# A streaming trunk on one core: the table work of the state-space layer dealt out over the first expert layer in another way

## The reference, cut to what matters

```python
D_MODEL = 1024; SEQ = 256; DEPTH = 2
N_EXPERT_GROUPS = 4; EXPERTS_PER_GROUP = 8; D_EXPERT = D_MODEL // 4
for i in range(DEPTH):
    hn = rms_norm(h, norm_mix[i])
    mix = chunked_rel_attention(...) if i % 2 == 0 else s5_mixer(...)
    h = h + mix
    hn = rms_norm(h, norm_ffn[i])
    h = h + hierarchical_moe(hn, ...)     # best group, best two experts in it
return rms_norm(h, norm_final)
# in hierarchical_moe:
for e in range(N_EXPERTS):
    hid = jax.nn.silu(t @ w_gate[e]) * (t @ w_up[e])
    out = out + gates[:, e:e + 1] * (hid @ w_down[e])
# in s5_mixer: x_k = abar * x_(k-1) + bbar u_k, y = Re(C x) + D u, scan over the positions
```

## Time and profile before

| what | us |
|---|---|
| time, median of 3 runs (lowest to highest) | 711.55 (710.52 to 712.64) |
| the profiled execution | 711.8 |
| its span, first to last instruction | 710.1 |
| busy: TensorE / VectorE / ScalarE / GpSimd | 629.6 / 193.9 / 136.7 / 190.2 |
| moved by DMA | 244.20 MB, 344 GB/s over the span |
| granted TensorE clock, mean share of full speed | 0.942 |

### The profile page before, as it was taken

One profiled execution on the slowest core, in us unless ns is written; L12 is line 12 of the kernel. 1 busy time (PEld: TensorE's weight loads), 2 busy tenths in 40 slices (PEclk: granted clock), 3 DMA queues, 4 the chain that ended last, 5 costly groups with the idle time before them and its releaser, 6 DMA issues.

```text
span 710.1 us, 13191 instructions
## 1 busy us (share of the span) xinstructions
PE 629.6 (89%) x5567; PEld 404.3 (57%) x5567; DVE 193.9 (27%) x499; ACT 136.7 (19%) x301; POOL 190.2 (27%) x226
## 2 busy tenths in 40 slices
PE   7999999999999988989598889999999798796583
PEld 5888888876556656456163654456564365353140
DVE  3234233254231023103022770235203023002003
ACT  3111313232021011011014511122220012010003
POOL 1001120250699997970961000030000000000001
PEclk9999999999998999899799999997999999898688
DMA  9997976665999999999999379964899999999992
GB/s 313 344 327 148 366 214 222 254 242 220 414 420 405 393 423 421 420 422 421 423 389 381 127 241 420 422 255 174 323 425 368 422 419 420 420 421 420 420 397 80
DMA packets 86707, 244.20 MB, mean 344 GB/s; under 512 B 28053, under 2 KB 56949, under 8 KB 62581
## 3 DMA queue, kind: packets, MB, share of 16 engines
q1 hardware_dynamic: 85188, 237.50, 86.7%
q0 software_dynamic: 1056, 5.24, 1.9%
q10 hardware_dynamic: 400, 0.57, 0.3%
HBM read 239.08 MB, written 4.22 MB: 343 GB/s over the span
## 4 chain that ended last, share of the span: by engine, by line
PE 72%; DMA 19%; SPq 3%; ACT 2%; DVE 1%; issue 1%; POOL 0%; DVEq 0%; POOLq 0%; ACTq 0%
DMA ring<-in_moe_w_down 11%; PE ps L2002 10%; DMA ring<-in_moe_w_up 9%; PE ps L1722 8%; PE ps L2289 8%; PE ps L2042 7%; PE ps L1856 7%; PE ps L2062 4%; PE ps L1725 4%; PE ps L1783 4%; PE ps L1702 3%; PE ps L1852 2%; SPq L478 2%; PE ps L1823 1%; PE ps L1918 1%
## 5 line engine op out<-in xcount | busy, mean ns | idle before, releaser
L2002 PE MATMUL ps<-ring,xg 128*32 128x256 f32 x1808 | 120.9, 402 | 26.3 <-DMA ring<-in_moe_w_up 14.5
L2002 PEld LDWEIGHTS ps<-ring,xg 128*32 128x32 f32 x1808 | 66.4, 116 | 74.3 <-issue 47.1
L2042 PE MATMUL ps<-ring,hidT 128*32 128x512 f32 x488 | 67.5, 671 | 15.8 <-DMA ring<-in_moe_w_down 10.6
L2062 PE MATMUL ps<-y_sb,pickT 128*128 128x512 f32 x128 | 59.5, 605 | 3.4 <-DVE y_sb L1475 1.7
L861 POOL TENSOR_TENSOR xh<-x,normw 128x1024 f32<-128x1024 f32 x1 | 2.4, 2352 | 214.2 <-DVE x L1437 214.2
L1722 PE MATMUL ps<-xnT,ring 128*128 128x256 f32 x256 | 57.7, 381 | 1.0 <-ACT xnT L904 1.0
L2289 PE MATMUL ps<-ring,yT 128*128 128x512 f32 x128 | 55.6, 594 | 0.9 <-ACT yT L1087 0.9
L1722 PEld LDWEIGHTS ps<-xnT,ring 128*128 128x128 f32 x256 | 47.8, 190 | 8.6 <-ACT xnT L904 1.2
L1442 DVE TENSOR_TENSOR hid<-sg,ps 128x256 f32<-128x256 f32 (+1 forms) x18 | 7.2, 399 | 156.2 <-ACT sg L1004 143.6
L2042 PEld LDWEIGHTS ps<-ring,hidT 128*32 128x32 f32 x488 | 17.4, 121 | 50.7 <-issue 43.3
L1856 PE MATMUL ps<-pick,xn 128*128 128x256 f32 x192 | 44.0, 382 | 0.0
(11 more groups left out here) (376 smaller groups left out, 878.1 us busy)
## 6 DMA issues: line engine op xcount, KB each, us to landing
ring<-in_moe_w_up SPq DMA_DIRECT2D x59, 1024.0 KB, 17.2
ring<-in_moe_w_gate SPq DMA_DIRECT2D x57, 1024.0 KB, 13.2
ring<-in_moe_w_down SPq DMA_DIRECT2D x53, 1024.0 KB, 16.2
ring<-in_attn_w_qkv SPq DMA_DIRECT2D x11, 1024.0 KB, 11.6
ring<-in_moe_w_down SPq DMA_DIRECT2D x16, 512.0 KB, 12.5
ring<-in_ssm_w_out SPq DMA_DIRECT2D x8, 1024.0 KB, 12.4
ring<-in_attn_w_o SPq DMA_DIRECT2D x4, 1024.0 KB, 10.9
chunk_inputs<-turned POOLq DMA_DIRECT2D x3, 1024.0 KB, 11.1
```

The costliest lines, as they stand in the source:

```text
L2002: ins = mm(ps[CAP * h:CAP * (h + 1), GUB, F * half:F * (half + 1)], p.xg[:, c, CAP * (ROUND * r + h):CAP * (ROUND * r + h + 1)], w, start= ...
L2042: ins = mm(ps[CAP * h:CAP * (h + 1), DNB + b, :], hidT[:, r, j, CAP * h:CAP * (h + 1)], w, start=(j == 0), stop=(j == FT - 1), tile_positi ...
L2062: ins = mm(ps[:, u, :], p.pickT[rows, r, tt * P:(tt + 1) * P], y_sb[rows, r, 512 * b:512 * (b + 1)], start=(r == 0), stop=(r == p.rounds - 1))
```

## The change: pieces in other rounds, lags among other products

Piece 0 stays in round 2. Piece 1 goes from round 4 to the spill, piece 2 from round 6 to round 4, and piece 3 from round 7 to round 6, so that round 7 has no table work. In rounds 2, 4 and 6 the lags are dealt out among the up products, one group of four before each eighth of them; in the spill among the gather products. The transposes follow at once, before the hidden values are turned. The copies of a piece are shared by ScalarE and VectorE for all four, and a store waits for the lags' copies by a semaphore of its own (`lags_evac`). In round 7 the sum of round 6 stands ahead of the gate products, and the warm block between gate and up. GpSimd's order is new too: `chunk_outputs(1)` goes behind the first store, `chunk_outputs(2)` stays in the second stretch, `steps` and the tables go behind `chunk_inputs(2)` and `(3)`.

```diff
 def piece(self, r):
+    if self.layer or self.layer is None or r:
+        return None
+    return 1 if self.spill else (None, 0, 2, 3)[self.octet]
...
             chunk_inputs(0)
-            chunk_outputs((0, 1))
+            chunk_outputs((0,))
             store_inputs(0)
             chunk_inputs(1)
-            chunk_outputs((2,))
-            steps()
-            tables((1, 2, 4, 8))
+            chunk_outputs((1, 2))
             store_inputs(1)
             chunk_inputs(2)
-            tables((16,))
+            steps()
+            tables((1, 2))
             store_inputs(2)
             chunk_inputs(3)
+            tables((4, 8, 16))
...
             def store_inputs(i):
+                pool.wait_ge(lags_evac, i + 1)
                 pool.wait_ge(tab_evac, 2 * (i + 1))
...
-                if r == 1 and p.layer == 0 and p.octet == NO - 1:
+                sums_first = p.layer == 0 and p.closes(r)
+                if sums_first:
                         pe.wait_ge(S.yh_done, p.k + r)
                         pe.wait_ge(S.yl_done, p.k + r)
-                        keep_warm(GUB, WARM["last lags"])
-                        lag_products(3, (DNB, DNB + 1)).then_inc(tab_turned, 1)
                         pe.wait_ge(before_p.S.x_added, 4 * before_p.n + 4)
-                        turn_chunk_inputs(0)
+                        combine(r - 1)
...
+                    if table:
+                        pe.wait_ge(tab_ready, p.piece(r) + 1)
...
                         loaded(r, second_full)
-                        gate_up(r, 1, S.gu_done)
+                        gate_up(r, 1, S.gu_done, p if table else None)
                     if final and after:
                         picked(after)
-                        gather(after, (0, 1))
+                        gather(after, (0, 1), beside=p if table else None)
+                    if table:
+                        pe.wait_ge(before_p.S.x_added, 4 * before_p.n + 4)
+                        turn_chunk_inputs(0)
...
                 def gate_up(r, half, done, beside=None):
                     for c in range(KT):
+                        if beside:
+                            lag_products(beside, (c,))
```

More of the change, by code:

```diff
@@ L72 @@
 FIRST_HEADS = 4
-WARM = {"start": 2, "choice": (5, 3), "ranks": 1, "regrouping": 1, "last lags": 4}
+WARM = {"start": 2, "choice": (5, 3), "ranks": 1, "regrouping": 1, "last up": 4}
 def trunk_program(nc, a, out):
@@ L993, in moe_act @@
                 for r in range(p.rounds):
[L994 to L1001, removed]
                     if not p.spill:
@@ L1010, in moe_act @@
                       .then_inc(S.hT_evac, 1)
+                    if p.piece(r) is not None:
+                        take_table(p.piece(r))
                     if after and r == p.rounds - 1:
@@ L1457, in moe_dve @@
                         hidden(after, 0, F // ROUND)
-                    if r == 0 and p.layer == 0:
-                        if p.table and p.table < 3:
-                            take_table(p.table, (GUB, HTB))
+                    if p.piece(r) is not None:
+                        take_lags(p)
+                        take_table(p.piece(r))
                     if r == 0:
@@ L1834, in router, with gather @@
                 pe.wait_ge(xn_ready, 4 * layer + 4)
-            def gather(p, us, halves=False):
+            def gather(p, us, halves=False, beside=None):
                 for u in us:
@@ L1980, in gate_ahead, with gate_up @@
                     ins.then_inc(q.S.first_done, 1)
-                def gate_up(r, half, done):
+                def gate_up(r, half, done, beside=None):
                     for c in range(KT):
+                        if beside:
+                            lag_products(beside, (c,))
                         if opens and (r, half, c) == (0, 0, KT // 2):
@@ L2095, in moe_pe @@
                             pe.wait_ge(S.x_added, 4 * p.n + 4)
-                        if p.layer == 0 and not p.table:
+                        if p.layer == 0 and p.octet == 0:
                             pe.wait_ge(const_evac, 2)
-                        if p.layer == 0 and p.closes(r):
-                            pe.wait_ge(tab_evac, 8)
-                        combine(r - 1)
+                        if sums_first:
+                            keep_warm(DNB, WARM["last up"])
+                        else:
+                            combine(r - 1)
                     elif before_p:
@@ L2103, in moe_pe @@
                         pe.wait_ge(before_p.S.yl_done, before_p.k + before_p.rounds)
-                    if r == 0 and p.layer == 0 and p.table == 3:
-                        lag_products(2, (DNB, DNB + 1))
-                        pe.wait_ge(before_p.S.x_added, 4 * before_p.n + 4)
-                        turn_chunk_inputs(0)
+                    table = p.piece(r) is not None
+                    if table and p.spill:
+                        pe.wait_ge(S.hid_ready, p.k + 1)
+                        pe.wait_ge(S.gslot_ready, p.gslots * (p.n + 1))
+                    if table:
+                        pe.wait_ge(tab_ready, p.piece(r) + 1)
                     if r == 0 and opens:
@@ L2149, in moe_pe @@
                             pe.wait_ge(before_p.S.x_added, 4 * before_p.n + 4)
-                        if p.layer == 0 and p.table:
-                            pe.wait_ge(tab_evac, 2 * p.table)
+                        if table:
+                            pe.wait_ge(tab_evac, 2 * p.piece(r) + 2)
                 if after and not early:
```

78 lines of the change are left out of this document (37 added, 41 removed).

## The result

The changed kernel takes 731.62 us (median of 4 runs, 730.56 to 732.37), the kernel before 711.12 us in the runs taken beside it (4 runs, 710.52 to 712.64). The ratio is 1.0277 with a 95% interval of 1.0246 to 1.0308: slower, and by some ten times the loss that I had forecast. The profiled execution of the changed kernel took 730.56 us. Its span is 18.6 us longer than that of before, so the two traces account for 18.6 of the 20.5 us between the medians.

What follows compares the result with a forecast made beforehand. The weights' stream was taken to set the pace of the first expert layer's rounds. Stream 4.7 us late, less 2.9 gained in round 7, made 1.8 us slower: 713.4 us, range 708.0 to 717.3.

Steps and rivals of the forecast that it cites:

- the loss that I had forecast: Whole kernel: 1.8 us slower, 713.4 us against a median of 711.55.
- a hole in it behind round 4: Weights' queue before round 5's ups: empty for 4.7 us, the stream late by that from there on.
- GpSimd's piece: Round 4: TensorE waits some 5.5 us for piece 2, which GpSimd finishes at 287.5.
- the transfers bound the gain there: Round 7: 6.6 us leave TensorE's chain, but the ups' landing at 368.1 limits the gain to 3.8 us.
- one of the signs that I had named for being wrong: Round 7: the prediction is wrong if TensorE does not wait for the ups.
- 5. Up and lags: 3.55 + 3.75, 1.4 for the pause, 0.4 for eight changes: 9.1 us.: Round 4: ups with dealt-out lags take 9.1 us, end at 296.6 and release round 5's ups.
- Rounds 2 and 6: nothing: Rounds 2 and 6: same table work beside products that wait for weights, so no time won or lost.
- the cover that would have to go: Rounds 2 and 6: waiting for weights hides lags and transposes; without it each round would cost about 6.6 us.
- Step 1: Spill: the earlier first store delays the gather's start by 0.8 us, from 259.87 to 260.7.
- the pause price of 0.9 in round 7: Round 7's ups: 0.9 us dearer after a pause of some 2.8 us, leaving 2.9 of 3.8 us gained.
- the second rival: Spill and round 4: tile changes cost 0.4 us per round trip, deciding from about 0.25; 717.6 us; chance 0.17.

Runs made afterwards that it cites:

- experiment 2: The changed kernel with unread blocks keeping TensorE warm in its pauses, 6 in round 4 and 5 in round 6: 721.55 us, 1.0137 of before.
- experiment 4: The kernel before without piece 3's lags and transposes, round 7 in the changed order: ups start 3.7 us earlier, second half 3.3; whole time not of use.
- experiment 5: The kernel before with 32 extra unread products of the lags' form dealt by fours among round 5's ups: 722.45 us, beside 712.61.
- experiment 6: The kernel before with 32 extra unread products of the lags' form in one run ahead of round 5's ups: 719.65 us, beside 712.61.
- experiment 9: The kernel before with eight unread blocks ahead of the spill's down product: 715.13 us, 1.0059 of before.
- experiment 1: The changed kernel with each piece's lags in one run ahead of the ups, or of the gather in the spill: 721.3 us, 1.0145 of before.
- experiment 11: The kernel before with eight unread blocks ahead of round 6's downs, the four ahead of round 7's lags kept: 709.92 us, 0.9988 of before.
- experiment 10: The kernel before with seven unread blocks ahead of round 6's downs, one instead of four ahead of round 7's lags: 708.15 us, 0.9962 of before.

## Why the prediction was wrong

**Right.** The queue sets the pace, and a hole in it behind round 4 is never given back; experiment 2 had that hole at about 5 us once the clock was right. Round 4 does wait for GpSimd's piece (5.97 us, forecast 5.5), and GpSimd's chain from the transposes' end to piece 2 took 17.5 us (273.31 to 290.78), forecast 17.3. Round 7's lags do leave the chain, and the transfers bound the gain there (experiment 4). But one of the signs that I had named for being wrong is in the trace: TensorE does not wait for the ups of round 7.

**The step that failed: "5. Up and lags: 3.55 + 3.75, 1.4 for the pause, 0.4 for eight changes: 9.1 us."** It measured 15.84. I took the price of a pause from a run of ups alone, in which the clock comes back after a while the earlier trace rows, and put it on a mixture in which it doesn't. Experiments 5 and 6 show the mixture's price without the table, experiment 2 shows the 8.97 us without the pause. A row that I passed over pointed there. Round 4 of the kernel before, lags and transposes:

```profile
280.67 4.57 PE L1918 MATMUL ps<-wC,wbt 64*128 64x16 f32 x64 [0.51 <-issue]
285.18 3.67 PE L1907 MATMUL ps<-ident_pad,wbt 128*128 128x128 f32 x16
```

Behind two short stops (1.05 and 0.51 us) the 64 lags took 4.57 us instead of 3.75 and the transposes 3.67 instead of 1.97, where I had looked only at round 6. With piece 2 finished at 290.78 instead of 287.5, the 15.84 us moved the ups' issue from 296.6 to 306.95. The last gate landed at 297.5 instead of 294.4, so the hole grew from 4.7 to 11.8 us.

**"Rounds 2 and 6: nothing"** failed for the same reason. Round 6 has the same pause (4.71 us, waiting for ups) and the same 15.84 us; it put TensorE 5.2 us behind the ups of round 7, where I had it ahead of them. I named the cover that would have to go and saw no sign of it, though the pause was to be read in the trace: in round 6 of the kernel before, the last up lands at 334.3, and the lags and transposes (329.65 to 335.3) stood between gates and ups and filled the wait. Dealt out among the ups, they no longer can.

**Step 1, 0.8 us for the early store,** was 3.4: the store lay beside round 3's ups, the last landed at 240.08 instead of 237.23, after the wait of 5.76 us their 64 records took 5.40 us instead of 3.66, and the spill's gather began at 263.25.

**What was not in the sum at all:** the spill's down product, 9.8 us late (277.89 instead of 268.07), holds back a ring slot, and its lateness pushes round 4's gates, which release round 5's. I followed the ups' release and not the gates' and downs'. Experiment 9 puts 4.3 us on it.

By size: the forecast for the span was +1.8, it was +18.6. The stream was 17.0 us late instead of 4.7 (12.3), TensorE was 5.2 us behind the ups instead of ahead, and the pause price of 0.9 in round 7 fell away: 16.6 of the 16.8.

**The tile changes.** Round 2 gives their price at the full clock: 8.96 us against 3.55 + 3.75 for the two runs, 1.66 over eight pairs or 0.21 us for going there and back; the spill's four pairs (8.15 us) give the same. So the second rival's mechanism was real, at half its price and below the 0.25 at which it was to decide; I had taken 0.05. The Trainium skill, "TensorEngine Tiling (Array Packing)", section "Key Properties", has the array drained at a change of tiling mode. These rows agree in that each change has a price, where the ones I had read did not show it; that draining is the reason, no run here shows.

## What to carry to other kernels

Before small products are dealt out among others, see whether TensorE has paused ahead of that place: the price of a pause is the price of what runs after it, and must be read from the same mixture, not from one of its parts. Work that is put ahead of a product counts at every load that this product and the next ones release: gates, ups and downs. The slack of such a load is its time to landing less that on an empty queue (here 8.7 less 5.0 us for the first gate of round 5). A queue that is never empty makes moved work look free until the first hole. And where the queue does hide it, as in experiment 6, look for the other engine that waits for the late work.

## What the runs showed of the hardware

- TensorE can be busy without a gap and stay at 1.2 GHz: granted clock 0.50 for 15.84 us while 64-row products of 16 columns alternated with 32-column-tile products of 256 columns (rounds 4 and 6, experiment 5). The Trainium skill, "TensorE: Matmul & The Clock Gate", section "What's actually happening", has the clock set by how busy TensorE has been recently. Here the profile's busy share (10.00 of 10 us in experiment 5, at 0.50) does not tell which level holds, and the measurement decides.
- A run of 64 such small products after a pause is slow throughout, 7.01 us (experiments 1 and 6). Even when it starts at full speed it can take the clock away from what follows (experiment 11: lags 3.75, transposes 3.61), but need not (round 6 of the kernel before: lags 3.75, transposes 1.97).
- Between 480 and 490 us, in the second layer's routing, whose instructions none of the edits touches, the granted clock was 0.59 (before), 0.70 (experiment 11) and 1.00 (experiment 10). Experiment 10's trace was 0.96 us ahead at 479.9 and 4.8 at 489.2. This is of the size of the spread between runs (708.13 to 715.86 for the kernel before beside experiment 11); whether it explains that spread stays open, since only one execution of each kernel has a trace.
